# Two transformer blocks on one core: prologue by quarters, late modulation loads in pairs, norm weights in ScalarE's copies, first 1/sum behind v

## The chip, the cores and the metric

One core of a Trainium2 chip runs the whole program. It has five engines with a queue each: TensorE (matmuls; PE in the profile, PEld its weight loads), VectorE (DVE), ScalarE (ACT), GpSimd (POOL) and SyncE (SP), which here only starts transfers. The metric is the device time of one execution in microseconds (us); lower is better.

## The reference, cut to what matters

Two blocks on x of 256 tokens by 2048, all in fp32. The first begins with a modulation: a vector c times a matrix w_ada of 2048 by 12288 (100 MB) gives shift, scale and gate of two norms.

```
c_act = silu(c);  sh1, sc1, gt1, sh2, sc2, gt2 = split(c_act @ w_ada + b_ada, 6)
h = rms_norm(x, g_norm1) * (1 + sc1) + sh1
q_d, k_d, v_d, cq, ckv, k_pe = split(h @ w_in)
q_d = rms_norm(q_d, g_q_diff);  k_d = rms_norm(k_d, g_k_diff)          # heads of 64
p1, p2 = softmax(q1 k1 / 8 + bias), softmax(q2 k2 / 8 + bias)          # 8 heads
a_out = rms_norm((p1 - lam * p2) @ v_d, g_subln) * (1 - lambda_init)
q_m = rope_tail(rms_norm(rms_norm(cq, g_q_a) @ w_q_b, g_q_mla))        # 8 heads of 128 + 64
k_m, v_m = ... @ w_kv_b (the same, with g_k_mla and the shared k_pe)
x = x + gt1 * (concat(a_out, softmax(q_m k_m) v_m) @ w_out)
h2 = rms_norm(x, g_norm2) * (1 + sc2) + sh2
x = x + gt2 * ((silu(h2 @ w_gate) * (h2 @ w_up)) @ w_down)
```

The second block (convolution branch, attention with forget gates, feed-forward, final norm) follows.

## The kernel before, in words

**Units.** Every weight matrix is streamed in loads of 1 MB into a ring of four buffers (raw). Each load is two units. For a unit ScalarE rounds 128x1024 numbers to w_hi (split, L1120 and L1133), VectorE forms the rest w_lo (L1645), and TensorE does twelve matmuls of 512 columns: hi by hi, lo by hi, hi by lo (unit, L615, L628). Units go through four slots and are split up to three units ahead. The results stand in three accumulators (acc).

**Modulation.** w_ada is read in 96 loads of 1 MB. For the first 80, TensorE multiplies a load with the columns of c (a "part", L658: four matmuls on 32 partitions each). Parts belong to groups; a finished group is copied to SBUF by VectorE (L1691, L1695) and turned into columns by TensorE (L673, L676), and VectorE adds the bias (L1717 to L1724). SEGMENTS says by which pieces of the 2048 rows of h the first 32 parts (NPRO) are grouped: each piece needs a group of sh1 and one of sc1. LEAD parts stand ahead of the first unit. These 32 loads have a ring of their own with four buffers (early_ada, L468); the later 48 go through raw between the weights, where GAPS says how many follow each load of weights. Each of the later 48 takes a PSUM bank alone and is added by VectorE (L1699, L1701). There are two such banks, used in turn by all transposes, parts, columns and attention products: their order is fixed, and a bank is used again only when its last reader is done.

**Order.** Each engine's program is written out by hand, and all follow the same tables: `prologue()` (L107) for what stands ahead of the first unit, `modulation(u)` (L124) for parts and columns behind unit u, `window(v)` (L378) for attention steps behind a unit, `heads_at` for the second attention. Segment 0 is units 0 to 11 (rows 0 to 1023 of h), segments 1 and 2 are units 12 to 17 and 18 to 23. The last part of the prologue's groups releases GpSimd's load of the bias table (L1603), which the mirror matmuls (L777) behind unit 17 and later read.

**Attention.** `qkN` (L1932) scales queries and keys by 1/rms and then by the weight g; `qbN` and `kvbN` (L1971, L1997) do the same for the second attention, with the rotation. TensorE transposes the result into a bank and ScalarE copies it out (bank_to, L1169). For a head of the first attention ScalarE does the exponentials (daE), `daW` (L2031) forms 1/sum for both softmaxes, scales the second, and subtracts; `dc` (L2044) copies the product with v out of its bank, ScalarE squares it, and `dcN` (L2051) does the norm.

## Time and profile before

| | |
|---|---|
| median of 3 runs | 2698.8 us (2695.52 to 2700.94) |
| the profiled execution | 2699.22 us, its span 2697.4 us |
| mean granted TensorE clock | 0.990 |
| TensorE busy | 2615.0 us (97%), 12162 matmuls |
| VectorE, ScalarE, GpSimd busy | 1583.7 (59%), 1163.8 (43%), 52.8 (2%) us |
| moved by DMA | 561.74 MB, mean 208 GB/s |
| matmuls of L628 in the chain that ended last | 83% of the span |

The page of the profile has the busy time of each engine, the chain of work that ended last, and the costliest groups of instructions. A span of matmul records is pipelined: a busy TensorE is one with no pause, not one at its peak. The trace behind it gives single instructions with the time that an engine stood idle before them and who released it.

### The profile page before, as it was taken

How to read it: one execution, taken by the hardware profiler on the slowest of the kernel's cores; microseconds unless marked ns; L12 is line 12 of the kernel's file. 1: busy time of each engine (PE TensorE's matmuls, PEld its weight loads, DVE VectorE, ACT ScalarE, POOL GpSimd, SP SyncE). 2: the span in 40 equal slices, each digit the busy share in tenths (PEclk: the TensorE clock that was granted, in tenths of full speed). 3: DMA queues.
4: the chain of work that ended last, by engine and by line, in shares of the span. 5: the costliest groups of instructions: out<-in, count | busy, mean ns of one | idle time of the engine just before them, and what ended most of it. 6: DMA issues, size and time to landing. Idle time of an engine off the chain costs nothing.

```text
span 2697.4 us, 32987 instructions
## 1 busy us (share of the span) xinstructions
PE 2615.0 (97%) x12162; PEld 2083.3 (77%) x12162; DVE 1583.7 (59%) x1755; ACT 1163.8 (43%) x1514; POOL 52.8 (2%) x84
## 2 busy tenths in 40 slices
PE   6999879989999999999999999999999999999997
PEld 2667656778888888887888877888888888888886
DVE  1467665657777555557755454556556565656565
ACT  2344444444333444443544455444444444444443
POOL 1010010000000000000000000000000000000000
PEclk9999989989999999999999999999999999999999
DMA  9967766647777655555655544665655555555552
GB/s 390 378 229 261 271 233 231 217 137 250 248 245 245 195 187 187 188 190 188 214 188 184 175 141 145 200 209 203 208 191 187 191 191 192 187 187 187 190 190 103
DMA packets 262819, 561.74 MB, mean 208 GB/s; under 512 B 9186, under 2 KB 13492, under 8 KB 261836
## 3 DMA queue, kind: packets, MB, share of 16 engines
q1 hardware_dynamic: 260688, 549.25, 60.4%
q0 software_dynamic: 1664, 9.19, 1.0%
q10 hardware_dynamic: 380, 2.13, 0.2%
q8 instruction: 57, 0.93, 0.1%
q14 instruction: 30, 0.25, 0.0%
HBM read 556.31 MB, written 4.21 MB: 208 GB/s over the span
## 4 chain that ended last, share of the span: by engine, by line
PE 91%; DVE 4%; DMA 2%; ACT 1%; issue 1%; POOL 0%; DVEq 0%; SPq 0%; POOLq 0%; ACTq 0%
PE acc L628 83%; PE bank L712 2%; PE bank L658 2%; DMA early_mix<-in_w_ada 2%; DVE w_lo L1645 1%; PE bank L862 1%; ACT w_hi L1133 0%; PE acc L853 0%; PE acc L1062 0%; PE acc L852 0%; PE acc L1061 0%; PE bank L724 0%; PE bank L686 0%; ACT probs L1340 0%; PE bank L676 0%
## 5 line engine op out<-in xcount | busy, mean ns | idle before, releaser
L1645 DVE TENSOR_TENSOR w_lo<-raw,w_hi 128x1024 fp32r<-128x1024 f32 x852 | 1037.9, 1225 | 816.3 <-ACT w_hi L1133 784.5
L1133 ACT ACTIVATE w_hi<-raw 128x1024 fp32r<-128x1024 f32 x852 | 901.3, 1060 | 1061.3 <-PE acc L628 960.7
L628 PE MATMUL acc<-w_hi,actT_hi 128*128 128x512 f32 (+1 forms) x2112 | 834.7, 395 | 1.2 <-DVE actT_lo L1783 0.8
L628 PE MATMUL acc<-w_hi,actT_lo 128*128 128x512 f32 (+1 forms) x2112 | 821.7, 389 | 0.0
L628 PE MATMUL acc<-w_lo,actT_hi 128*128 128x512 f32 (+1 forms) x2112 | 821.5, 389 | 0.0
L628 PE MATMUL acc<-w_hi,mixT_hi 128*128 128x512 f32 (+1 forms) x1280 | 503.5, 393 | 8.5 <-DVE mixT_lo L1773 5.4
L628 PE MATMUL acc<-w_hi,mixT_lo 128*128 128x512 f32 (+1 forms) x1280 | 498.0, 389 | 0.0
L628 PE MATMUL acc<-w_lo,mixT_hi 128*128 128x512 f32 (+1 forms) x1280 | 497.2, 388 | 0.0
L628 PEld LDWEIGHTS acc<-w_hi,actT_hi 128*128 128x128 f32 x2112 | 397.9, 188 | 115.0 <-issue 25.8
L628 PEld LDWEIGHTS acc<-w_hi,actT_lo 128*128 128x128 f32 x2112 | 397.8, 188 | 83.0
L628 PEld LDWEIGHTS acc<-w_lo,actT_hi 128*128 128x128 f32 x2112 | 398.3, 189 | 79.0 <-issue 1.0
L628 PEld LDWEIGHTS acc<-w_hi,mixT_hi 128*128 128x128 f32 x1280 | 241.0, 188 | 72.1 <-issue 13.5
L628 PEld LDWEIGHTS acc<-w_hi,mixT_lo 128*128 128x128 f32 x1280 | 240.7, 188 | 49.6
L628 PEld LDWEIGHTS acc<-w_lo,mixT_hi 128*128 128x128 f32 x1280 | 241.0, 188 | 47.5
L2142 DVE TENSOR_TENSOR x_res<-x_res,acc 128x1024 f32<-128x1024 f32 x68 | 83.1, 1221 | 30.5 <-PE acc L628 30.5
L658 PE MATMUL bank<-raw,ccol 128*32 128x512 f32 x384 | 54.0, 641 | 11.7 <-DVEq L1722 5.6
L712 PE MATMUL bank<-cst,work 128*128 128x128 f32 x356 | 47.7, 273 | 11.0 <-DVEq L1705 3.9
L712 PEld LDWEIGHTS bank<-cst,work 128*128 128x128 f32 x356 | 41.5, 140 | 19.5 <-issue 6.3
L1180 ACT ACTIVATE mixT_hi<-bank 128x512 fp32r<-128x512 f32 (+1 forms) x54 | 25.6, 504 | 64.7 <-PE bank L712 40.6
L2142 DVE TENSOR_TENSOR wide<-wide,acc 128x1024 f32<-128x1024 f32 x36 | 44.0, 1221 | 14.5 <-PE acc L628 14.5
L1434 ACT ACTIVATE work<-acc,kpe 128x512 f32<-128x512 f32 x48 | 30.4, 686 | 39.3 <-PE acc L628 39.3
L1576 POOL TENSOR_SCALAR rstd<-ss 128x2 f32<-128x2 f32 (+2 forms) x27 | 7.6, 283 | 1965.6 <-DVE ss L1803 1713.7
(270 smaller groups left out, 1128.6 us busy)
## 6 DMA issues: line engine op xcount, KB each, us to landing
raw<-in_w_ff SPq DMA_DIRECT2D x128, 1024.0 KB, 5.1
raw<-in_w_in SPq DMA_DIRECT2D x108, 1024.0 KB, 5.1
raw<-in_w_ada SPq DMA_DIRECT2D x64, 1024.0 KB, 5.0
raw<-in_w_gate SPq DMA_DIRECT2D x44, 1024.0 KB, 5.1
raw<-in_w_up SPq DMA_DIRECT2D x44, 1024.0 KB, 5.1
raw<-in_w_down SPq DMA_DIRECT2D x44, 1024.0 KB, 5.0
early_mix<-in_w_ada SPq DMA_DIRECT2D x16, 1024.0 KB, 9.5
wide<-in_w_ada SPq DMA_DIRECT2D x16, 1024.0 KB, 8.8
```

The source lines that it names most:

```text
L628: last_mm = pe.matmul(acc[p][:, t, 0:width], act[x][:, k0 + c, t * P:(t + 1) * P], w[:, u % SPL, c * NW:c * NW + width], start=first and c ...
L658: ins = pe.matmul(dst[32 * j:32 * j + 32, :], ccol[:, 2 * r + j // 2 if n_ == 8 else 4 * r + j, :], src[:, j * NW:(j + 1) * NW], start=alo ...
L712: ins = pe.transpose(bank[b][:, j * P:(j + 1) * P], src_of(j), ident)
L862: ins = pe.matmul(bank[b][:, 0:S], v[:, k, h * P:(h + 1) * P], attT[:, k, :], start=(k == 0), stop=(k == 1))
L1133: act.activation(w_hi[:, u % SPL, :], raw[:, ld % RAW, (u % DU) * 1024:(u % DU + 1) * 1024], ACT.Copy) \
L1180: act.activation(dst, bank[b][:, 0:n], ACT.Copy).then_inc(bank_hi, 1)
L1434: ins = act.activation(stg[:, t * NW:(t + 1) * NW], acc[p][:, t, :], ff, scale=scale[:, t:t + 1])
L1576: link(pool.tensor_scalar(slot, ss[:, 0:n], 1.0 / width, EPS, ALU.mult, ALU.add))
L1645: dve.tensor_tensor(w_lo[:, u % SPL, :], raw[:, ld % RAW, (u % DU) * 1024:(u % DU + 1) * 1024], w_hi[:, u % SPL, :].bitcast(F32), ALU.subt ...
L2142: link(dve.tensor_tensor(dst[:, :, g * NW:(g + 1) * NW], dst[:, :, g * NW:(g + 1) * NW], acc[g % 2][:, :, :], ALU.add))
```

## The change

Six edits. (1) The first segment is halved, so that four segments of 512 rows each are left: LEAD falls from 16 to 8, a segment is six units, and behind its units 0 to 3 stand 1, 2, 2 and 3 parts of the next one; SyncE asks for 3, 3 and 2 of these behind each load of weights. The copies of gains, the transposes of x, the first splits and the modulation of the first columns are mixed in one list. (2) The later 48 parts come as 24 pairs, spread over loads 12 to 50; a pair adds up in one bank and VectorE takes it once. (3) The weights of the norms of queries and keys are no longer multiplied in by VectorE: ScalarE's copy out of the bank takes them as its scale, and the rotated part has them in its tables (turns_q). (4) The first softmax is left unscaled: the weights become p1 + p2 * (-lam * sum1 / sum2), and 1/sum1 comes with the norm behind v. (5) The product with v is copied by ScalarE, after its squares, and no longer by VectorE. (6) b_f_2 is loaded apart, later, by GpSimd.

```diff
-SEGMENTS = ((0, 8), (8, 4), (12, 4))
+SEGMENTS = ((0, 4), (4, 4), (8, 4), (12, 4))
-GAPS = [0] * 12 + [1] * 16 + [2] * 9 + [1] * 14 + [0] * 3
+EARLY_GAPS = (3, 3, 2)
+EARLY_AT = (1, 2, 2, 3, 0, 0)
+GAPS = [0] * 12 + [2 * ((i + 1) * 24 // 39 - i * 24 // 39) for i in range(39)] + [0] * 3
@@ prologue()
-        if 5 <= a < 13:
-            steps.append(("x", 2 * (a - 5)))
-        if a == 13:
-            steps.append(("gains",))
-        if a == 14:
-            steps.append(("rows",))
-    steps += [("columns", n) for n in completed(LEAD - 1)]
-    return steps + [("part", LEAD), ("part", LEAD + 1)]
+        if a == 3:
+            steps += [("gains",), ("rows",)]
+        if a >= 4:
+            steps.append(("x", 2 * (a - 4)))
+    steps += [("x", 8), ("columns", 1), ("modulated", 0), ("split",), ("split",), ("x", 10), ("modulated", 1)]
+    return steps + [("x", 12), ("x", 14), ("split",)]
@@ modulation(u)
-        return [LEAD + 1 + v] if 0 < v < NPRO - LEAD - 1 else []
+        if not 0 <= v < 18:
+            return []
+        first = LEAD + v // 6 * 8 + sum(EARLY_AT[:v % 6])
+        return list(range(first, first + EARLY_AT[v % 6]))
@@ TensorE, part_sums
+                begins, ends = (r == 0, r == n_ - 1) if a < NPRO else (a % 2 == 0, a % 2 == 1)
...
-                                    src[:, j * NW:(j + 1) * NW], start=alone or r == 0,
-                                    stop=alone or r == n_ - 1)
+                                    src[:, j * NW:(j + 1) * NW], start=begins, stop=ends)
@@ ScalarE
-            def bank_to(dst, n=NW, shape=None):
+            def bank_to(dst, n=NW, shape=None, weight=None):
...
-                act.activation(dst, src, ACT.Copy).then_inc(bank_free[b], 1)
+                scale = 1.0 if weight is None else cols2[:, ROWS2[weight][0]:ROWS2[weight][0] + 1]
+                act.activation(dst, src, ACT.Copy, scale=scale).then_inc(bank_free[b], 1)
@@ ScalarE, dc
-                skip_banks(1)
-                act.wait_ge(oc_ready, h + 1)
+                b = next_bank()
                 before_sums()
                 for t in range(TT):
-                    ins = act.activation(sq[:, t * P:(t + 1) * P], ostg[:, t, :], ACT.Square, accum_out=ss[:, t:t + 1])
+                    ins = act.activation(sq[:, t * P:(t + 1) * P], bank[b][:, t * P:(t + 1) * P], ACT.Square,
+                                         scale=rr[:, t:t + 1], accum_out=ss[:, t:t + 1])
                 ins.then_inc(ss_ready, 1)
+                act.activation(ostg.rearrange("p t d -> p (t d)"), bank[b][:, 0:TT * P], ACT.Copy) \
+                    .then_inc(bank_free[b], 1)
@@ VectorE, part_sums
-                if a < NPRO and not last_of_group(a):
+                if (a < NPRO and not last_of_group(a)) or (a >= NPRO and a % 2 == 0):
                     return
@@ VectorE, qkN; qbN; kvbN
-                g_ = (gq, gk)[g // 2][:, :].unsqueeze(1).broadcast_to([P, 16, 64])
-                dve.tensor_tensor(stg.rearrange("p (a d) -> p a d", d=64), stg.rearrange("p (a d) -> p a d", d=64), g_,
-                                  ALU.mult).then_inc(stg_ready, 1)
...
-                link(dve.tensor_tensor(s4, s4, gqm[:, :].unsqueeze(1).broadcast_to([P, 4, QKH]), ALU.mult))
...
-                free(p)
-                dve.tensor_tensor(s4, s4, gkm[:, 0:P].unsqueeze(1).broadcast_to([P, 4, P]), ALU.mult)
...
                 dve.wait_ge(stg_ready, L.next("stg"))
+                free(p)
                 inv_rms_used()
@@ VectorE, daW
-                link(dve.tensor_scalar(rr[:, 2:4], rr[:, 2:4], lam[:, 0:1], None, ALU.mult))
-                for t in range(TT):
-                    ins = dve.tensor_scalar(probs[:, 2 + t, :], probs[:, 2 + t, :], rr[:, 2 + t:3 + t], None, ALU.mult)
-                link(ins)
-                for t in range(TT):
-                    ins = dve.scalar_tensor_tensor(out=attw[:, t, :], in0=probs[:, t, :], scalar=rr[:, t:t + 1],
-                                                   in1=probs[:, 2 + t, :], op0=ALU.mult, op1=ALU.subtract)
+                link(dve.scalar_tensor_tensor(out=rr[:, 2:4], in0=rr[:, 2:4], scalar=lam[:, 0:1], in1=rs[:, 0:2],
+                                              op0=ALU.mult, op1=ALU.mult))
+                for t in range(TT):
+                    ins = dve.scalar_tensor_tensor(out=attw[:, t, :], in0=probs[:, 2 + t, :], scalar=rr[:, 2 + t:3 + t],
+                                                   in1=probs[:, t, :], op0=ALU.mult, op1=ALU.add)
@@ VectorE, the first 24 units
-                for q in modulated_at(u - 1):
+                for q in modulated_at(u):
```

How TensorE's queue changes ahead of the first unit. L658 (now L665) is a part, L724 (L730) a transposed pair of x, L673 and L676 (L682) the columns of a group, L770 (L775) the gains, L628 (L635) a matmul of a unit. Before, from product 12 on (L757 is the turning of the second set of rows):

```order
L658 MATMUL acc<-early_mix,ccol 32x512 x4
L724 MATMUL bank<-rt,x_res 128x128 x4
L658 MATMUL acc<-early_mix,ccol 32x512 x4
L770 MATMUL bank<-probs,ones 128x512
L770 MATMUL bank<-probs,ones 128x392
L658 MATMUL acc<-wide,ccol 32x512 x4
L757 MATMUL bank<-cst,tmp 128x104
L658 MATMUL acc<-wide,ccol 32x512 x4
L673 MATMUL bank<-sel,part 128x2 x4
L658 MATMUL bank<-early_mix,ccol 32x512 x8
L628 MATMUL acc<-w_hi,actT_hi 128x512
```

and now, from product 5 on:

```order
L665 MATMUL acc<-early_mix,ccol 32x512 x4
L730 MATMUL bank<-rt,x_res 128x128 x4
L665 MATMUL acc<-wide,ccol 32x512 x4
L730 MATMUL bank<-rt,x_res 128x128 x4
L665 MATMUL acc<-wide,ccol 32x512 x4
L730 MATMUL bank<-rt,x_res 128x128 x8
L682 MATMUL bank<-ones,part 128x1 x4
L730 MATMUL bank<-rt,x_res 128x128 x12
L635 MATMUL acc<-w_hi,actT_hi 128x512
```

Sixteen products and the first two of the next group (L658 into bank, x8) stood ahead of the first unit; now eight do, and three of the eight transposed pairs stand behind the columns.

SyncE's queue, where the late loads of w_ada go through the ring raw. Before, where w_in ends:

```order
L451 DMA raw<-in_w_in 128x4x512
L451 DMA raw<-in_w_ada 128x2x1024
L451 DMA raw<-in_w_in 128x4x512
L451 DMA raw<-in_w_ada 128x2x1024
L451 DMA raw<-in_w_in 128x4x320
L451 DMA raw<-in_w_ada 128x2x1024 x2
L451 DMA raw<-in_w_in 128x4x320
```

and now:

```order
L458 DMA raw<-in_w_in 128x4x512 x2
L458 DMA raw<-in_w_ada 128x2x1024 x2
L458 DMA raw<-in_w_in 128x4x512
L458 DMA raw<-in_w_in 128x4x320
L458 DMA raw<-in_w_ada 128x2x1024 x2
L458 DMA raw<-in_w_in 128x4x320
L458 DMA raw<-in_w_ada 128x2x1024 x2
```

Before, one load of w_ada followed each load of weights, and two followed each of nine; now it is two or none all through, with one or two loads of weights between (here one load of 512 columns and one of 320 stand together).

VectorE's queue at a head of the first attention with the norm of keys: L2034 to L2040 are daW (now L2030 to L2034), L1936 and L1942 are qkN (now L1937 alone), L1701 (L1706) the sum of a part, L1645 (L1653) a w_lo. Before:

```order
L1701 TENSOR_TENSOR part<-part,bank 128x512
L1645 TENSOR_TENSOR w_lo<-raw,w_hi 128x1024
L1936 TENSOR_TENSOR work<-acc,rstd 128x1024
L1942 TENSOR_TENSOR work<-work,gains 128x1024
L2034 RECIPROCAL rr<-rs 128x4
L2035 TENSOR_SCALAR rr<-rr,lam 128x2
L2037 TENSOR_SCALAR probs<-probs,rr 128x256 x2
L2040 SCALAR_TENSOR_TENSOR att<-probs,rr 128x256 x2
L1645 TENSOR_TENSOR w_lo<-raw,w_hi 128x1024
L1773 TENSOR_TENSOR mixT_lo<-bank,mixT_hi 128x256
L1701 TENSOR_TENSOR part<-part,bank 128x512
```

and now:

```order
L1653 TENSOR_TENSOR w_lo<-raw,w_hi 128x1024 x2
L1937 TENSOR_TENSOR work<-acc,rstd 128x1024
L2030 RECIPROCAL rr<-rs 128x4
L2031 SCALAR_TENSOR_TENSOR rr<-rr,lam,rs 128x2
L2034 SCALAR_TENSOR_TENSOR att<-probs,rr 128x256 x2
L1653 TENSOR_TENSOR w_lo<-raw,w_hi 128x1024
L1778 TENSOR_TENSOR mixT_lo<-bank,mixT_hi 128x256
L1706 TENSOR_TENSOR part<-part,bank 128x512
```

The product with the weights, the two scalings of the second softmax and the sum of a part ahead are gone from here; the sum behind is left (L1773, now L1778, is the low half of a finished head).

## Rows read from the trace of the kernel before

**Rows 1.** Windows by stretch: us, busy (x instructions) of each engine, PEclk, DMA share, GB/s.

```profile
60.00:133.00 73.00, 72.96 (x369) 46.88 (x370) 31.20 (x42) 27.95 (x35) 1.01 (x1) 0.97 1.01 386
...
280.00:345.00 65.00, 54.94 (x360) 38.81 (x359) 44.88 (x79) 27.83 (x76) 5.77 (x11) 0.95 0.79 279
345.00:410.00 65.00, 49.17 (x248) 32.42 (x247) 44.22 (x86) 30.20 (x102) 10.69 (x17) 0.89 0.66 229
410.00:500.00 90.00, 88.94 (x428) 60.96 (x427) 46.03 (x79) 36.70 (x69) 0.00 (x0) 1.00 0.67 230
```

**Rows 2.** The chain of waits: start, us, engine, tile and line.

```profile
61.98 7.02 PE acc L628 x24
...
70.00 2.95 PE acc L628 x12
...
122.67 1.00 PE bank L658 x8
...
126.62 0.79 PE bank L676 x8
...
154.31 5.67 PE acc L628 x24
```

**Rows 3.** Timeline ahead of the first unit: start, us, instruction, idle before it.

```profile
31.98 1.07 PE L658 MATMUL acc<-wide,ccol 128*32 128x512 f32 x8
...
32.97 1.16 PE L724 MATMUL bank<-rt,x_res 128*128 128x128 f32 x8
...
39.89 1.06 PE L658 MATMUL acc<-wide,ccol 128*32 128x512 f32 x8 [0.30 <-DMA wide<-in_w_ada]
...
42.33 1.06 PE L658 MATMUL acc<-wide,ccol 128*32 128x512 f32 x8 [0.29 <-DMA wide<-in_w_ada]
...
44.52 0.60 ACT L1174 ACTIVATE xT<-bank 128x512 f32<-128x512 f32 x1 [1.85 <-PE bank L724]
...
54.78 2.00 ACT L1133 ACTIVATE w_hi<-raw 128x1024 fp32r<-128x1024 f32 x2 [7.22 <-DMA raw<-in_w_in]
...
56.69 1.08 ACT L1251 ACTIVATE xT<-xT,mcol 128x256 f32<-128x256 f32 x2
```

**Rows 4.** The page's DMA issues: size of each, median us to landing.

```profile
raw<-in_w_ada SPq DMA_DIRECT2D x64, 1024.0 KB, 5.0
```

**Rows 5.** Timeline: the issue of the bias table, and the first mirror matmul.

```profile
124.72 1.01 POOL L1603 DMA_DIRECT2D wide<-bias_by_distance  x1 [103.46 <-DVE part L1695]
...
132.84 1.02 PE L777 MATMUL bank<-wide,att 128*128 128x512 f32 x2
```

**Rows 6.** The tile of the bias table, 110 to 140 us: from issue to landing.

```profile
DMA to landing us min/median/max: 7.2/7.2/7.2
```

**Rows 7.** VectorE's groups by shape, 165 to 410 us: busy us, mean ns; idle before.

```profile
L1701 DVE TENSOR_TENSOR part<-part,bank 128x512 f32<-128x512 f32 x31 | 21.2, 685 | 7.2 <-PE bank L658 5.7
...
L2037 DVE TENSOR_SCALAR probs<-probs,rr 128x256 f32<-128x256 f32 x16 | 4.9, 351 | 0.3
```

**Rows 8.** Timeline near 200 us: the weights of the keys, and TensorE behind them.

```profile
199.28 1.23 DVE L1942 TENSOR_TENSOR work<-work,gains 128x1024 f32<-128x1024 f32 x1 [0.24 <-DVE work L1936]
...
204.04 1.22 PE L712 MATMUL bank<-cst,work 128*128 128x128 f32 x8 [1.23 <-DVE mixT_lo L1773]
```

**Rows 9.** The chain of waits near 364 us.

```profile
364.52 0.97 DVE work L1983
```

**Rows 10.** Windows of 2 us, columns as in rows 1.

```profile
320.00:322.00 2.00, 0.00 (x0) 0.00 (x0) 1.76 (x6) 0.00 (x0) 0.00 (x0) 0.54 1.02 383
322.00:324.00 2.00, 1.96 (x9) 0.33 (x9) 0.69 (x1) 0.97 (x1) 0.00 (x0) 0.50 1.05 416
```

**Rows 11.** Timeline: two parts that came together, and their sums.

```profile
310.64 1.92 PE L658 MATMUL bank<-raw,ccol 128*32 128x512 f32 x16
...
315.44 1.51 DVE L1701 TENSOR_TENSOR part<-part,bank 128x512 f32<-128x512 f32 x2
```

**Rows 12.** Waits from 340 to 400 us: us in total, times, longest.

```profile
PEld bank L658 <- DMA raw<-in_w_ada: 2.8, 2, 1.8
```

More of the change, by code:

```diff
@@ L453, in load @@
                 if kind == "w":
-                    for _ in range(2):
+                    for _ in range(EARLY_GAPS[(ORDER[:n[0]].count("w") - 1) % 3]):
                         if asked[0] < NPRO:
@@ L765, in gain_columns @@
             def gain_columns():
[L767 to L771 removed]
+                pe.wait_ge(gain_in, 16 * 4)
+                b, _ = wait_bank()
+                pe.matmul(bank[b][:, 0:NW], ones[0:1, :], gains_row[:, 0:NW], start=True, stop=True) \
+                    .then_inc(bank_full[b], 1)
             def mirror_chunk(n_):
```

143 lines of the change are left out of this document (68 added, 75 removed).

## Prediction

> **What bounds the kernel now.** The page first: TensorE is busy for 97% of the span, as the table of the profile shows, so only three things can save time: work taken from TensorE, a start that comes sooner, and pauses that close. The windows by stretch say where pauses are [rows 1]. From 410 to 500 us, and from 500 on as well, TensorE hardly stops. From 280 to 410 it is busy 54.94 of 65 and 49.17 of 65 us, so 25.9 us of pause lie there, while VectorE has 44.88 and 44.22 us of work in the same stretches; the granted clock falls to 0.95 and 0.89 too. The chain of waits says how the run starts: loads of the modulation matrix until 61.98 us, when the first two units run (a unit is 12 matmuls of 128x512), then a steady pattern: product of a part 1.00, unit 2.95, and 0.79 for turning a finished group into columns [rows 2]. In that stretch the DMA engines are full (share 1.01, 386 GB/s) and TensorE is too (72.96 of 73 us) [rows 1].
>
> **Prologue by quarters.** Eight products instead of sixteen now stand ahead of the first unit, and the two of the next group that stood there are gone as well. Before, product 7 ran at 31.98 and took 1.07 [rows 3], so it ends at 33.0; now it is the last one needed. Behind it stand two transposed pairs at 1.05 (1.16 with the overlap) and the columns, 1.0: 36.2. VectorE turns these into the scale, 0.7; ScalarE then does two of its 128x256 products (1.08), two w_hi copies (2.00) and one bank copy (0.60), which frees the bank that the last transposed pair waits for: 40.6, and 1.2 for the pair. First unit at 41.9, 20 us sooner [rows 2, 3]. Most of this is work that only changes places: from there a segment of six units carries eight products and two columns. Six units are four at 2.95 and two at 2.72 (a unit behind a unit is cheaper: two behind a product take 5.67 [rows 2]), products 8 x 1.0, columns 2 x 0.79: 26.8 us. Product 31 ends after two segments, four units, eight products and one group of columns: 41.9 + 53.6 + 20.6 = 116.1.
>
> The loads need about the same: a load of 1 MB comes each 2.45 us (the products at 39.89 and 42.33, each waiting for its load) [rows 3], eleven per segment are 27.0. And the four early buffers are used harder: load 15 may be asked for only when product 11 is done (three units and four products, 54.8), takes 5.0 alone [rows 4] and more behind another, so it lands at 60 to 62, while TensorE comes to it at 61.5. I take 1.1 us of wait in each of three segments: product 31 ends at 119.5. Now a new wait shows. GpSimd asks for the bias table when the last part is summed; before, its issue stood at 124.72, 1.05 behind product 31 (ended 123.67), and it landed 7.2 later [rows 2, 5, 6], 8.3 us after the product. The mirror matmul at 132.84 found it there, having three units and columns between (9.2 us) [rows 5]. Now two units and columns stand between: 6.7 us, so TensorE waits 1.6 and the mirror runs at 127.8, 5.0 sooner than before. Half a us I take back for the clock of the first units and for the shorter path from a segment's last columns to its next unit, two units less than before. Term: -4.5. Ends: -8 (no wait on loads, table landed), +1 (load waits of 3 us in each segment).
>
> **ScalarE takes the norm weights.** The copy out of the bank (0.60 for 512 columns [rows 3]) gets a scale, which I price at nothing: it replaces a constant in the same instruction (ends 0 and 0.1 us each). VectorE loses one 128x1024 product of 1.23 for each of four groups [rows 8], one 128x768 of 0.97 for each of four query pairs [rows 9], and one 128x512 of 0.69, the size of a sum [rows 7], for each of four key pairs. The first kind decides once: at 199.28 it runs, and at 204.04 TensorE has stood 1.23 us waiting for that row of VectorE's work [rows 8]. Term: -1.2 (ends 0, -1.3). Elsewhere before 280 TensorE has cover enough.
>
> **1/sum behind v.** Each of eight heads loses two scalings of 351 ns [rows 7] with their wait; the bank copy moves to ScalarE, +0.4 for each head ahead of its next w_hi (256 columns; bounds 0.3, half of the 0.60, and 0.6), and is no longer waited for before the squares.
>
> **The stretch 280 to 410.** The chain there runs through VectorE, row by row; the 0.97 us of the query weights at 364.52 is one such row [rows 9]. On the chain stand four of these (-3.9), three heads' scalings (3 x 0.7 = -2.1), and two second sums of a part (2 x 0.8 = -1.6). The pairs also take products away: of 48 parts 18 stood at units 54 to 70, now 12. Six products less of 1.0 on a path that they share half of the time: -3.0. Against it ScalarE's longer step twice (+0.8) and the later release of the key sums (+0.6, since now the bank is given back behind three VectorE operations). -9.2 in all; other paths come forward where a chain is cut, and I take two thirds: -6.0. Ends: 0 and -14.
>
> **Late loads in pairs.** The six products go where TensorE is the bound. There a lone product costs 1.0 and makes the next unit dearer by 0.23, a pair costs 2.15. Units 22 to 52: 16 x 1.2 = 19.2 before, 9 x 2.15 + 0 = 19.4 now; units 72 to 98: 14 x 1.2 = 16.8, now 19.4. Term: +2.7 (ends +1, +5). VectorE does 24 sums instead of 48 of 0.69 [rows 7], hidden here behind 88.94 of 90 us of matmuls [rows 1].
>
> **Sum.** -4.5 -1.2 -6.0 +2.7 = -9.0. The profiled execution took 2699.2 us (the span of 2697.4 and 1.8 around it), 0.4 above the median of the runs. 2690.
>
> **Rivals.**
> The stretch opens (B). VectorE has 12 sums less (8.3), four query weights (3.9), four key weights (2.8), five heads' scalings (3.5) and bank copies (1.6), 20 of its 89 us there; the pauses may go below the point where the clock falls. The clock means 0.95 and 0.89 over 65 us each are 10.4 us of full-speed cycles [rows 1]; a window at 0.50 stands there [rows 10]. If two thirds of this come back and the cut chain counts in full, it is -9.2 and -7 in place of -6: 2680. For it: VectorE is the bound there for many rows of the chain. Against: ScalarE and GpSimd steps stand on the same chain and stay.
> The Trainium skill (TensorE: Matmul & The Clock Gate, "Part 1: The HAM clock gate") says that an idle TensorE is throttled to half rate and that activity releases it. By that rule, shorter pauses pay twice; the trace agrees, the 0.50 follows a window without any matmul [rows 10].
>
> Little is left (C). The loads set the pace: at the mean 386 GB/s of 60 to 133 us instead of 430, a load of 1.05 MB takes 2.72, the 33 loads behind product 7's end at 122 at the earliest, 2.5 later, and the stretch gives only half: -2, -1.2, -3, +2.7: 2696. For it: DMA share 1.01. Against: the same engines brought a load each 2.45 us at 40 us [rows 3].
> The Trainium skill (DMA: Bandwidth & Descriptors, "Bandwidth") puts HBM to SBUF at about 358 GB/s for a core. An estimate by that page of the Trainium skill is 2.93 us for a load, 33 of them 97 us, and the mirror at 138, 5 us later than before. The measured 386 to 430 contradict it, so it gets no chance of its own.
>
> Slower (D): the pairs starve. Where two pairs follow each other (nine places: units 28/30, 38/40, 44/46, 54/56, 64/66, 70/72, 80/82, 90/92, 96/98) the second part of the second pair can be asked for only when the first pair is summed, and part and sum are now released together. It lands 5.0 + 0.5 behind the sum [rows 4]; TensorE has two units (5.7), one product (1.0) and at least 1 us of head work until it needs it, 7.7. It decides when the sum comes more than 2.2 us behind the pair. Where VectorE is free the sum ends 0.7 behind its product, but the two sums at 315.44 end at 316.95, 4.4 behind their products (312.56) [rows 11]; the longest wait of the weights of a product for its load is 1.8 there [rows 12]. Nine times 1.8 are 16: 2706. For it: VectorE's order. Against: only two or three of the nine lie where VectorE is late, and there it is relieved.
>
> **Chances.** Forecast 0.50, B 0.25, C 0.16, D 0.07, others 0.02. What the measurement tells from no change is 0.2%, 5.4 us. Faster than 2693.4: most of the forecast (0.46), B and a little of C: 0.74. The same: 0.18. Slower: 0.08. The range for 8 in 10 holds forecast, C and nearly all of B: 2676 to 2699.
>
> **What would show it.** First unit at 41 to 43 us (wrong above 46). TensorE waits for an early load once in each segment, near 1 us; over 3 means C. The first mirror matmul waits for the bias table, 1 to 3 us, and runs at 126 to 130. No wait of TensorE for w_lo near 200. From 280 to 410: pauses of 15 to 20 instead of 25.9 us; below 12 with the clock at 0.97 or more means B. Waits of TensorE for raw loads from w_ada of more than 5 us in all mean D. Behind 550 us nothing should differ by more than 1 us; if it does, the forecast has left something out.

## The result, and the profile after

| | before | after |
|---|---|---|
| median | 2698.34 us (2695.52 to 2700.94) | 2709.78 us (2706.27 to 2712.43) |
| ratio, 95% interval | | 1.0042 [1.0029, 1.0055] |
| the profiled execution, its span | 2699.22, 2697.4 | 2706.27, 2704.2 |
| first matmul of the first unit | 61.91 | 42.19 |
| first product of group 2 (behind unit 0) | | 45.12 |
| first mirror matmul | 132.84 | 155.3 |
| first matmul of w_kv_b (L905 before, L910 after) | 371.3 | 374.3 |
| first transpose of the second norm | 546.5 | 553.7 |

The change made the kernel 0.42% slower, 11.4 us by the medians and 7.0 by the two profiled executions. The table of times shows three parts: 22.5 us are lost up to the mirror matmul, 19.5 won from there to w_kv_b (238.5 us before, 219.0 after), 4.2 lost again up to the second norm. Behind that the two differ by 0.4 us in all: the span ends 6.8 us later. The kernel before was run again beside every set of experiments; its median was 2698.34 us here, and 2699.91 (e1 to e4), 2700.47 (e5 to e8), 2699.22 (e9 to e12) and 2699.32 (e13 to e15) later, so a difference between two sets can be off by 2 us.

The first table is the windows of the kernel after, with the stretches of [rows 1] (us, busy and instructions of PE, PEld, DVE, ACT, POOL, then granted clock, DMA share and GB/s).

```profile
60.00:133.00 73.00, 60.65 (x304) 35.83 (x304) 23.65 (x32) 18.67 (x24) 0.00 (x0) 0.91 0.86 317
280.00:345.00 65.00, 62.60 (x393) 48.09 (x392) 44.98 (x74) 35.39 (x82) 5.75 (x10) 1.00 0.76 266
345.00:410.00 65.00, 52.00 (x284) 38.49 (x283) 37.87 (x81) 35.38 (x122) 12.83 (x22) 0.92 0.68 231
410.00:500.00 90.00, 90.00 (x447) 62.91 (x444) 43.16 (x74) 37.49 (x71) 0.00 (x0) 1.00 0.70 252
```

From 60 to 133 us TensorE was busy for 72.96 of 73 us before [rows 1] and is for 60.65 now, and the DMA engines, full before (1.01), are at 0.86. Neither TensorE nor the loads bound this stretch any more: something makes both wait. From 280 to 410 the pauses are 15.4 us instead of 25.9. These windows are fixed in time while the work in them has moved by some us, so a part of the difference may be the shift.

Next, the timeline of TensorE ahead of the first unit, the counterpart of [rows 3]. The last transposed pair ends at 42.4, and the first unit begins at 42.19: forecast 41.9.

```profile
36.05 1.02 PE L682 MATMUL bank<-ones,part 128*128 128x1 f32 x8
36.93 2.03 PE L730 MATMUL bank<-rt,x_res 128*128 128x128 f32 x16
41.27 1.16 PE L730 MATMUL bank<-rt,x_res 128*128 128x128 f32 x8 [2.31 <-ACT xT L1180]
45.12 1.07 PE L665 MATMUL bank<-early_mix,ccol 128*32 128x512 f32 x8
```

Then the timeline of SyncE (SPq: its queue; start, time until all of the row are issued, waits within the row included, line), and of the other engines in the same place. L488 are early loads of w_ada, L458 loads of weights, L1704 is VectorE's copy of a finished group, L682 TensorE's columns of it.

```profile
50.60 0.51 SPq L458 DMA_DIRECT2D raw<-in_w_in  x1
51.15 12.27 SPq L488 DMA_DIRECT2D wide<-in_w_ada  x2
63.47 0.51 SPq L458 DMA_DIRECT2D raw<-in_w_in  x1
```
```profile
58.98 2.00 ACT L1138 ACTIVATE w_hi<-raw 128x1024 fp32r<-128x1024 f32 x2 [11.79 <-DMA raw<-in_w_in]
60.07 2.36 DVE L1653 TENSOR_TENSOR w_lo<-raw,w_hi 128x1024 fp32r<-128x1024 f32 x2 [11.44 <-ACT w_hi L1138]
62.35 0.68 DVE L1704 COPY part<-bank 128x512 f32<-128x512 f32 x1
63.23 1.35 PE L682 MATMUL bank<-ones,part 128*128 128x1 f32 x8 [4.42 <-DVEq L1710]
70.69 2.01 ACT L1138 ACTIVATE w_hi<-raw 128x1024 fp32r<-128x1024 f32 x2 [9.71 <-DMA raw<-in_w_in]
```

This is the loss. Read it from the bottom up: ScalarE waits 9.71 us for weights that SyncE asked for only at 63.47. In front of them in SyncE's queue stood early load 15 (the second of the two that begin at 51.15), whose buffer product 11 had used. Product 11 is the last of its group, so SyncE waits for VectorE's copy of the sum, not for the product. That copy (62.35) stands on VectorE behind w_lo of units 4 and 5 (60.07), and w_lo waits for weights that landed late (58.98), since SyncE asked for them only at 50.60, behind early load 13, which waits for product 9 in unit 1. So a late load of weights delays the copy, the copy delays the next load, and that one comes late again. From 60 to 63 us no matmul runs and almost nothing is transferred (10 GB/s), as the window shows:

```profile
60.00:63.00 3.00, 0.00 (x0) 0.00 (x0) 2.93 (x3) 0.98 (x2) 0.00 (x0) 1.00 0.02 10
```

The waits of SyncE from 40 to 155 us (us in total, times, longest), and the two sides that pay for them:

```profile
SPq L488 <- PE bank L665: 44.1, 10, 9.4
SPq L488 <- DVE part L1704: 39.7, 5, 11.4
```
```profile
ACT w_hi L1138 <- DMA raw<-in_w_in: 70.3, 9, 11.8
PE bank L682 <- DVEq L1710: 16.1, 6, 4.4
```
```profile
SPq L481 <- PE bank L658: 24.5, 8, 4.8
SPq L481 <- DVE part L1695: 12.9, 3, 4.3
```

The last two lines are the kernel before: the same wait for the copy is there, three times, never over 4.3 us. After, the wait comes at each group's end. The first products of the segments stand at 45.12, 81.58 and 117.46, 36 us apart. GpSimd asks for the bias table at 145.6 (124.72 in [rows 5]), it takes 9.6 us to land (7.2 in [rows 6]), and the mirror matmul waits for it, 2.8 us, until 155.3.

### The profile page after: what moved, and what is told of

Same layout as the page of the kernel before. It is cut to its first block, busy times and chain, and to the rows that moved or that the text cites. A ratio compares the mean times of both kernels' runs of the same rounds, so it can differ in the third digit from the quotient of the medians.

```text
span 2704.2 us, 33011 instructions
## 1 busy us (share of the span) xinstructions
PE 2616.4 (97%) x12176; PEld 2091.4 (77%) x12176; DVE 1550.7 (57%) x1711; ACT 1167.0 (43%) x1522; POOL 53.8 (2%) x86
## 4 chain that ended last, share of the span: by engine, by line
PE 83%; DVE 2%; ACT 1%; issue 1%; DMA 0%; POOL 0%; DVEq 0%; POOLq 0%; ACTq 0%
PE acc L635 77%; PE bank L718 2%; PE bank L665 1%; PE bank L867 1%; DVE w_lo L1653 0%; PE acc L858 0%; PE acc L1067 0%; PE acc L857 0%; PE acc L1066 0%; PE acc L910 0%; PE bank L730 0%; DMA raw<-in_w_ada 0%; PE bank L692 0%; DVE wide L2162 0%; DVE x_res L2166 0%
## 5 line engine op out<-in xcount | busy, mean ns | idle before, releaser
L1653 DVE TENSOR_TENSOR w_lo<-raw,w_hi 128x1024 fp32r<-128x1024 f32 x852 | 1037.6, 1225 | 874.0 <-ACT w_hi L1138 843.5
L635 PE MATMUL acc<-w_hi,actT_hi 128*128 128x512 f32 (+1 forms) x2112 | 835.6, 396 | 1.7 <-DVE actT_lo L1788 0.8
L635 PE MATMUL acc<-w_hi,actT_lo 128*128 128x512 f32 (+1 forms) x2112 | 822.9, 390 | 0.0
L635 PE MATMUL acc<-w_lo,actT_hi 128*128 128x512 f32 (+1 forms) x2112 | 822.6, 389 | 0.0
L635 PE MATMUL acc<-w_hi,mixT_hi 128*128 128x512 f32 (+1 forms) x1280 | 503.9, 394 | 9.6 <-DVE mixT_lo L1778 4.3
L635 PE MATMUL acc<-w_hi,mixT_lo 128*128 128x512 f32 (+1 forms) x1280 | 498.3, 389 | 0.0
L635 PE MATMUL acc<-w_lo,mixT_hi 128*128 128x512 f32 (+1 forms) x1280 | 497.8, 389 | 0.0
L635 PEld LDWEIGHTS acc<-w_hi,actT_hi 128*128 128x128 f32 x2112 | 398.3, 189 | 104.7 <-issue 19.8
L635 PEld LDWEIGHTS acc<-w_hi,actT_lo 128*128 128x128 f32 x2112 | 398.1, 188 | 83.1
L635 PEld LDWEIGHTS acc<-w_lo,actT_hi 128*128 128x128 f32 x2112 | 398.6, 189 | 80.1 <-issue 1.5
L635 PEld LDWEIGHTS acc<-w_hi,mixT_hi 128*128 128x128 f32 x1280 | 241.1, 188 | 70.1 <-issue 13.1
L635 PEld LDWEIGHTS acc<-w_hi,mixT_lo 128*128 128x128 f32 x1280 | 241.1, 188 | 49.5
L635 PEld LDWEIGHTS acc<-w_lo,mixT_hi 128*128 128x128 f32 x1280 | 241.4, 189 | 47.5
L665 PE MATMUL bank<-raw,ccol 128*32 128x512 f32 x384 | 47.4, 600 | 8.2 <-DMA raw<-in_w_ada 5.8
L1682 DVE SCALAR_TENSOR_TENSOR part<-raw,ccol,part 128x512 f32<-128x512 f32 x60 | 45.1, 751 | 1.7
```

Source lines behind the costliest of these rows:

```text
L635: last_mm = pe.matmul(acc[p][:, t, 0:width], act[x][:, k0 + c, t * P:(t + 1) * P], w[:, u % SPL, c * NW:c * NW + width], start=first and c ...
L665: ins = pe.matmul(dst[32 * j:32 * j + 32, :], ccol[:, 2 * r + j // 2 if n_ == 8 else 4 * r + j, :], src[:, j * NW:(j + 1) * NW], start=beg ...
L1653: dve.tensor_tensor(w_lo[:, u % SPL, :], raw[:, ld % RAW, (u % DU) * 1024:(u % DU + 1) * 1024], w_hi[:, u % SPL, :].bitcast(F32), ALU.subt ...
L1682: ins = dve.scalar_tensor_tensor(out=part[:, :], in0=src, scalar=ccol[:, k, 0:1], in1=part[:, :], op0=ALU.mult, op1=ALU.add)
```

## Experiments

**The two halves of the change.** The first run puts the prologue of before into the changed kernel, the second the new prologue alone into the kernel before:

```diff
-SEGMENTS = ((0, 4), (4, 4), (8, 4), (12, 4))      # e1; e2 is the reverse
+SEGMENTS = ((0, 8), (8, 4), (12, 4))
-EARLY_GAPS, EARLY_AT = (3, 3, 2), (1, 2, 2, 3, 0, 0)
+EARLY_GAPS = (2, 2, 2);  early(v) = [LEAD + 1 + v] if 0 < v < NPRO - LEAD - 1 else []
```

> The changed kernel with the prologue of before put back (one group pair of 8 chunks, then two of 4; 16 early products ahead of the first unit; two early loads behind each weights load); norm weights, softmax change and pairs of late loads stay. Theory T (the new prologue holds itself up: SyncE's early load waits for VectorE's copy of a finished group, the copy stands behind w_lo, w_lo waits for a weights load that SyncE only asks for behind that early load): the mirror row is back near 132.8 us from 155.3, and all behind it keeps its gain over before, so about 2687 us (2683 to 2690). Rival T2 (the stretch from the mirror to 371 us gained 19.5 us only because it had fallen behind and caught up with loads that had run ahead): the mirror is back too, but behind it only some 7 us are gained and 4 lost, about 2695 us (2692 to 2698). Rival R (the prologue was not the loss): 2705 us or more.

Measured 2684.87 us, ratio to before 0.9945 [0.9932, 0.9959]. The mirror is back at 132.9, and the stretch to w_kv_b takes 218.4 us, as in the changed kernel (219.0). T holds; T2 falls, the gain behind the mirror is no catching up. The changed kernel is 24.9 us above this one by the medians, 26.5 if each is held against the kernel before of its own set.

> The kernel before with the new prologue alone (quarters, weights mixed in, three, three and two early loads behind each weights load); late loads single, norm weights on VectorE, softmax as before. Theory T, the parts simply add: mirror row near 155, 2698 + 22 = 2720 us (2716 to 2723). Rival T2 (a late prologue is partly caught up between the mirror and 371 us whatever the rest is): mirror near 155, but 2708 us (2705 to 2712). Rival R (the prologue was not the loss): 2690 to 2699.

Measured 2730.44, ratio 1.0119 [1.0103, 1.0134]: 30.5 us over before, mirror at 161.0, 5.7 later still than in the changed kernel. T's sign and place hold, its range (2716 to 2723) does not: "simply add" was too low by 10 us. The rest of the change takes 4 to 6 us off what this prologue costs. Which part does was not tried.

**The links of the circle, one at a time.** Order on VectorE's queue (e3), release of the early buffer (e4), order on SyncE's queue (e5):

```diff
@@ e3: VectorE, unit(), for the first 17 units
-                split();  run(todo);  modulation events
+                run(todo);  modulation events;  split()
@@ e4: SyncE, early_ada(), where product `used` is the last of its group
-                        sp.wait_ge(part_ready, sums_by(used))
+                        sp.wait_ge(bank_full[b], m)        # the product itself
@@ e5
-EARLY_GAPS = (3, 3, 2)
+EARLY_GAPS = (3, 1, 4)
```

> The changed kernel, but in the first 17 units VectorE takes a unit's modulation work (the copy of a finished group, the columns) ahead of the split of the unit three further on, instead of behind it. Theory T: the copy no longer waits for a weights load that SyncE asks for behind the early load that waits for the copy; SyncE's waits for that copy fall from 39.7 us to under 10, a segment takes some 28 us instead of 36, mirror row near 130, 2684 to 2692 us. Rival L (the loads themselves set the pace of the prologue, 28 MB asked in another order): segments stay near 36 us, mirror over 150, 2706 us or more.

Measured 2703.36, 1.0010 [0.9999, 1.0020]: 6.4 us better than the changed kernel, mirror 147.7. Outside T's range, and not L's either. By the order of the code it removes one step only: in unit 1 the split of unit 4 already stands ahead of unit 2's copy, and both halves of a load wait for the same landing. No run tried that alone. SyncE's waits for the copy fell to 30.9 us, where T had said under 10:

```profile
SPq L488 <- DVE part L1708: 30.9, 5, 10.4
```

> The changed kernel, but an early load whose buffer was last read by the last product of a group waits for that product (its bank being full) instead of for VectorE's copy of the sum; the copy itself stays behind w_lo. Theory T: this cuts the circle at its other link, so the weights loads come on time and w_lo with them; the copy is then late only by the units that VectorE splits ahead; SyncE waits for products only, mirror row 130 to 140, 2685 to 2697 us. Rival Q (the order on VectorE's queue is the whole cost, SyncE's wait only follows it): mirror over 148, 2703 us or more. Rival L (the loads' own pace): 2706 or more.

Measured 2701.83, 1.0010 [1.0000, 1.0019], mirror 147.5: 8.0 us better, at the poor end between T and Q. The wait for the copy is gone from SyncE, but the waits for products grew from 44.1 to 70.0 us:

```profile
SPq L489 <- PE bank L666: 70.0, 14, 10.3
```

TensorE's columns still wait for the copy behind w_lo (11.0 us in all, 16.1 in the changed kernel), and the third weights load of a segment stands behind load 13, which waits for product 9.

> The changed kernel with one table altered: behind the weights loads of a segment 3, 1 and 4 early loads are asked instead of 3, 3 and 2, so the third weights load no longer stands behind early load 13, which waits for product 9 in the second unit. Theory T, widened by what the two runs before showed (each of the two cuts alone gave 7 us): SyncE asks the third weights load of each segment only at 50.6 us and it lands near 60, when unit 4 wants it; asked 12 us earlier, that stall of 4 to 6 us in each of three segments goes, the circle by the copy may still hold the next load: mirror 134 to 146 instead of 155, 2687 to 2699 us. Rival L (DMA bytes set the pace): 2705 or more.

Measured 2693.11, 0.9972 [0.9962, 0.9982], 16.7 us better and in T's range: two early loads moved from ahead of the third load of weights to behind it are worth more than either cut. Mirror 144.9, in a profiled execution that was the slowest of nine (2701.02). The wait for the copy is still there, five times, but no longer than 4.3 us:

```profile
SPq L488 <- DVE part L1704: 21.0, 5, 4.3
```

**All three, and whether quarters gain at all.**

> The changed kernel with all three repairs: early loads asked 3, 1 and 4 behind the weights loads, VectorE's modulation work ahead of its split in the first 17 units, and the early load released by the product rather than by VectorE's copy. Theory T: with no wait left that goes through a load asked later, the prologue by quarters gives what the prediction gave it: mirror 126 to 131, 2679 to 2685 us, some 5 us below the run with the old prologue. Rival L (in the kernel before the DMA share is 1.01 from the start to 123 us, so the loads bound the prologue in either order): mirror 131 to 135 and 2684 to 2689, no better than the old prologue. Rival S (a fourth wait is behind these): over 2692.

Measured 2686.67, 0.9944 [0.9931, 0.9956]; the mirror stands at 138.4 in the profiled execution, which took 2694.4 and was the slowest of the five. By its time that is L, not T; the mirror is later than either said. To settle it, three kernels ran on one chip, this one again, one with 3, 2, 3 in the table, and the old prologue again:

> The kernel with all three repairs, but early loads asked 3, 2 and 3 behind the weights loads of a segment instead of 3, 1 and 4. In the trace of the 3, 1, 4 run the DMA queue runs dry once, share 0.26 and 0.32 in the two stretches 48 to 51 and 51 to 54 us, because every load that needed no product had been asked by then; 3, 2, 3 leaves one more early load ahead of the third weights load. Theory D (the prologue by quarters is bound by its bytes: 28.4 us a segment for 11 loads of 1 MB, so only dry stretches can be won): mirror within 3 us of the 3, 1, 4 run and 2683 to 2688 us. Theory C (the circle returns through early load 12, which waits for product 8 ahead of the third weights load): 2690 or more.

> The kernel with all three repairs once more, beside the one with the old prologue on the same chip. Theory Q (quarters, once repaired, gain what the prediction gave them, 4.5 us): 4 us or more below the old prologue. Theory D (bytes bind both): within 3 us of it, and the mirror row no more than 2 us earlier than 132.9 us.

> The changed kernel with the prologue of before, once more, beside the one with all three repairs on the same chip: 2683 to 2687 us by every theory, mirror at 132.9; it is the base that the other two are held against.

Measured 2688.33 (0.9964 [0.9950, 0.9978], mirror 134.4), 2684.94 (0.9949 [0.9935, 0.9962], mirror 130.8) and 2682.16 (0.9942 [0.9929, 0.9956], mirror 132.7). Q falls: the repaired quarters reach the mirror 1.9 us sooner than e15 and gain nothing in the end, 2.8 us above the old prologue with intervals that overlap. D's time is met and its mirror limit, 2 us before 132.9, missed by 0.1. Its reason, the bytes, is only a part of it, as the rows of e14 below show. The 3, 2, 3 run lies just between D and C by its time and its mirror. The dry stretch it was to close is in it as well (share 0.47 from 45 to 48 us) and is missing in e14, so it belonged to one execution and not to the order.

The profiled executions differ in when their first unit starts, for a reason of its own (see "What the runs showed of the hardware"). From there to the mirror (us):

| | first unit | mirror | between |
|---|---|---|---|
| forecast | 41.9 | 127.8 | 85.9 |
| the changed kernel | 42.2 | 155.3 | 113.1 |
| e2, new prologue alone | 45.0 | 161.0 | 116.0 |
| e3, copy first | 42.2 | 147.7 | 105.5 |
| e4, early released | 41.2 | 147.5 | 106.3 |
| e5, weights earlier | 47.2 | 144.9 | 97.7 |
| e6, all three | 46.8 | 138.4 | 91.6 |
| e13, all three, 3, 2, 3 | 43.2 | 134.4 | 91.2 |
| e14, all three again | 40.7 | 130.8 | 90.1 |

So e6, e13 and e14 are alike within 1.5 us, and the place of one early load (3, 2, 3 or 3, 1, 4) makes no difference that shows. The timeline and a window of e14:

```profile
43.67 1.07 PE L666 MATMUL bank<-early_mix,ccol 128*32 128x512 f32 x8
...
72.05 1.06 PE L666 MATMUL bank<-early_mix,ccol 128*32 128x512 f32 x8
...
100.15 1.07 PE L666 MATMUL bank<-early_mix,ccol 128*32 128x512 f32 x8
```
```profile
60.00:133.00 73.00, 64.02 (x351) 39.76 (x348) 29.25 (x42) 22.83 (x30) 1.00 (x1) 0.97 1.04 405
```

The first product of each segment comes 28.4 and 28.1 us behind the last, with eleven loads of 1.05 MB in between: 409 GB/s, and the window shows a share of 1.04 at 405 GB/s. TensorE is nearly full too: from 43.67 to 100.15 it is busy for 54.0 of 56.5 us. It waits for an early load once in each segment, 1.0 us each time, 3.0 in all, which is what the forecast gave a segment (26.8 us of work and 1.1 of wait). Of the 9 us of pause in the window most is one wait for the bias table:

```profile
119.73 1.00 POOL L1611 DMA_DIRECT2D wide<-bias_by_distance  x1 [99.77 <-DVE part L1709]
130.79 2.07 PE L783 MATMUL bank<-wide,att 128*128 128x512 f32 x2 [5.46 <-DMA wide<-bias_by_distance]
```

GpSimd asks for the table at 119.73, 4.8 us sooner than in e15 (124.57) and 0.8 sooner than forecast. But the table takes 11.0 us to land (11.3 in e6, 11.0 in e13), against 7.2 in e15. So 3.8 of the 4.8 us are lost in its landing. The DMA engines are fuller while it is under way, a share of 1.04 from 119.7 to 130.8 us against 0.85 in e15 from 119.0 to 132.7; that this makes the landing longer fits, but no run changed it alone. The last 1.9 us are gone at the second norm: from w_kv_b to there e14 takes 183.0 us, e15 179.4. In e6 and e13 it is 179.6 and 179.3, so this belongs to the one execution. The Trainium skill (DMA: Bandwidth & Descriptors, "Bandwidth") puts HBM to SBUF at about 358 GB/s for a core while both cores of a pair stream, and at 425 for one core alone with 16 MB; an estimate from the first is 32.2 us for a segment's eleven loads. The run, a program on one core, has 28.2, which is nearer to the second.

**Where the gain behind the mirror is from.** The pairs taken out of e1, and put alone into the kernel before:

```diff
-GAPS = [0] * 12 + [1] * 16 + [2] * 9 + [1] * 14 + [0] * 3          # before; e7
+GAPS = [0] * 12 + [2 * ((i + 1) * 24 // 39 - i * 24 // 39) for i in range(39)] + [0] * 3
-    start, stop = True, True; one bank and one addition for each late part
+    start, stop = a % 2 == 0, a % 2 == 1; one bank and one addition for two      # e8
```

> The first of these runs (changed kernel, prologue of before) with the late modulation loads single again, in the places of before, each product with its own bank and its own addition. Theory P+ (pairs cost, the prediction's +2.7: their first loads wait for the pair's sum): 2682 us (2680 to 2684). Theory P- (pairs gain: one pass of VectorE fewer per two loads, 24 of 685 ns, and banks open for less): 2690 us or more. 2684 to 2687 means that they do nothing.

> The kernel before with the late loads in pairs alone (places and sums), prologue, norm weights and softmax as before. Theory P+: 2702 us (2700 to 2704). Theory P-: 2695 or less. If P- holds on one base and P+ on the other, the pairs are worth something only where VectorE is the late party, which the norm weights and the softmax change relieve as well.

Measured 2699.56 (0.9995 [0.9986, 1.0004]) and 2690.23 (0.9963 [0.9950, 0.9976]). P- holds on both bases: the pairs are worth 10.2 us alone (medians 2690.23 and 2700.47) and 14.7 with the rest (e1 against e7, of two sets; 14.1 against the kernel before of each), while norm weights and softmax without them are worth nothing that can be measured. Three runs take the pairs apart, the first two with one bank and one addition per part:

```diff
@@ e9: pair places, single sums
+GAPS as in e8;  everything else as before
@@ e10: single sums, spread evenly
+GAPS = [0] * 12 + [(i + 1) * 48 // 39 - i * 48 // 39 for i in range(39)] + [0] * 3
@@ e11: the pairs of e8, VectorE
+                    ins = dve.tensor_tensor(part[:, :], part[:, :], part[:, :], ALU.max)
```

> The kernel before, with only the places of the late modulation loads changed to those of the pairs (two behind one weights load, 24 times, spread over 39 weights loads); every product keeps its own bank and its own addition on VectorE. The pairs as a whole, alone on this base, gave 2690.2 against 2700.5. Theory Pl (the gain is the spreading: before, nine loads in a row carry two, in the stretch that ends near 330 us): 2690 to 2694 us. Theory Su (the gain is the shared bank and the pass of VectorE that is saved): 2698 us or more.

> The kernel before, with its 48 late loads spread evenly over 39 weights loads, one or two behind each, and single sums. Theory Pl: 2690 to 2694 us, like the pair places. Theory Su: 2697 to 2702. Rival E (two loads behind one weights load are what hurts, wherever): evenly spread singles below the pair places by 2 us or more.

> The pairs alone on the kernel before, and VectorE makes one more pass of 128x512 per pair (the maximum of the sum with itself, in place), so it makes as many passes as with single sums, while the bank is still filled once per pair. Theory V (the pass saved is the gain, since VectorE is late for TensorE between 280 and 410 us): 2697 us or more. Theory Bk (the bank taken once instead of twice, or the places): 2690 to 2693 us.

Measured 2698.70 (0.9999 [0.9990, 1.0008]), 2694.94 (0.9981 [0.9972, 0.9989]) and 2688.10 (0.9959 [0.9948, 0.9971]). V falls, Su holds for e9, and E for e10; e11 is 2 us below the range of Bk. VectorE's saved passes are worth nothing that shows: e11 makes as many as before and is as fast as e8. The places alone are worth nothing either, two single sums behind one load undo what the spreading gives (E: evenly spread singles are 3.8 better). What is left between e9 and e11, which have the same places and the same number of passes, is 10.6 us for what the shared bank brings: it is taken once instead of twice, and VectorE stops once, behind the second product. These two were not taken apart. The busy time and idle time of TensorE's products from the mirror to w_kv_b, before, e9 and e11:

```profile
L658 PE MATMUL bank<-raw,ccol 128*32 128x512 f32 x272 | 38.2, 643 | 10.5 <-DVEq L1722 5.6 <-DVE mixT_lo L1773 2.3 <-ACT q_nope L1174 1.7
```
```profile
L658 PE MATMUL bank<-raw,ccol 128*32 128x512 f32 x240 | 30.8, 615 | 8.9 <-DVE mixT_lo L1773 7.4 <-DMA raw<-in_w_ada 0.9 <-ACT x_res L1174 0.3
```
```profile
L660 PE MATMUL bank<-raw,ccol 128*32 128x512 f32 x240 | 29.4, 599 | 2.8 <-DMA raw<-in_w_ada 2.3 <-ACT x_res L1175 0.3
```

With a bank for each part, a product waits until VectorE has emptied the bank it takes next (5.6 and 2.3 us before, 7.4 in e9). With one bank for two, that wait is gone in e11 and 1.1 us in e8; what remains is the load. The transposes, which take banks from the same two, do not gain but wait a little longer. TensorE's waits in this stretch for a bank that VectorE had to empty, in us:

| | before | e9 | e8 | e11 |
|---|---|---|---|---|
| products of parts | 7.9 | 7.4 | 1.1 | 0 |
| transposes | 7.4 | 7.8 | 8.9 | 9.1 |

The whole stretch from mirror to w_kv_b, in one window each, of before, e9, e8 and e11:

```profile
132.80:371.30 238.50, 217.71 (x1194) 153.18 (x1194) 165.86 (x254) 106.70 (x232) 27.39 (x32) 0.97 0.73 255
```
```profile
132.60:364.10 231.50, 211.97 (x1155) 155.34 (x1154) 161.40 (x248) 107.11 (x236) 27.10 (x32) 0.96 0.68 243
```
```profile
132.50:356.70 224.20, 208.48 (x1155) 151.56 (x1154) 152.16 (x233) 106.64 (x232) 26.27 (x32) 0.98 0.71 252
```
```profile
133.50:356.20 222.70, 208.79 (x1156) 154.21 (x1154) 160.89 (x247) 106.58 (x232) 27.43 (x32) 0.98 0.72 253
```

Of the 14.3 us between before and e8, 9.2 are busy time of TensorE (30 products instead of 34 stand there, 30.8 us instead of 38.2) and 5.1 are pause, as much as the table gives. The four products are not saved: they come behind w_kv_b, where e8 takes 3.4 us more up to the second norm, so 10.9 are left, near the 10.2 of the medians.

The two traces of e9 and e11 need care. The one of e9 is of its fastest execution of eleven (2695.06), the one of e11 of the second slowest of six (2694.76, where four took 2685.6 to 2689.8), and their spans are equal, 2693.3 and 2693.0 us. What e11 gains up to w_kv_b, 8.8 us, it loses from there to the second norm: 185.5 us at a granted clock of 0.94, against 178.7 at 0.98 in e9 and 178.6 at 0.97 in e8. The 10.6 us stand on the medians. Whether the added pass causes the slow executions of e11 stays open.

**Softmax or norm weights.** Edits (4) and (5) of the change on top of e8:

```diff
-attw = p1 * rr1 - (p2 * rr2);  dc copied by VectorE, then squared
+attw = p1 + p2 * rr2';  dc squared by ScalarE from the bank with scale rr1, then copied by it
```

> The pairs alone plus the change to the first softmax (1/sum behind v, ScalarE squares and copies dc's bank); norm weights stay on VectorE. With norm weights as well the run gave 2684.9, with the pairs alone 2690.2. Theory X (the softmax change carries these 5 us, it shortens the heads' chain): 2684 to 2687 us. Theory N (the norm weights carry them): 2689 to 2691 us.

Measured 2686.14, 0.9955 [0.9942, 0.9967]: inside X's range, 4.1 us below e8 and 1.3 above e1, but the three intervals overlap. In the traces the stretch from mirror to w_kv_b is 224.2, 221.4 and 218.4 us with the pairs alone, with softmax, and with both.

## Why the prediction was wrong

**Prologue by quarters: -4.5 forecast, +22.5 at the mirror.** This is the step that failed. The first unit came as worked out (42.2 for 41.9), with luck in it, since eight executions with this prologue have it between 40.7 and 47.2. The arithmetic of a segment, 26.8 us for TensorE and 27.0 for the loads, was near the 28.2 that the repaired kernel takes. What failed is "I take 1.1 us of wait in each of three segments": a segment took 36.5 and 35.9 us. The prediction saw that load 15 needs product 11, and put its issue at 54.8. It was issued behind 62.35, because SyncE waits for VectorE's copy. Neither that copy's place behind w_lo nor what stands behind load 15 in SyncE's queue (the next weights) was followed: the wait for the copy, 39.7 us of SyncE's time in all, was put at nothing without a reason. The loss is three waits linked through two queues written in order: cutting one gave 6 to 17 us, all three 23 and 25.

Repaired, the term is nought: 2684.94 against 2682.16. There the waits for loads are as forecast (1.0 us a segment) and product 31 ends at 118.7, forecast 119.5. The step that failed is the landing of the bias table, taken as 7.2 us from the kernel before: it took 11.0, TensorE waited 5.5 us for it instead of 1.6, and the mirror stood at 130.8, not 127.8. The loads' rate, read at 40 us as one each 2.45, was 2.56 in the segments (28.2 by 11).

**Norm weights: -1.2.** Right at its place, not told from nothing in the time. The rows are the transposes of the same keys in e12 (weights still on VectorE), in e1 and in the changed kernel; [rows 8] has 1.23 us of wait before them.

```profile
203.86 1.22 PE L713 MATMUL bank<-cst,work 128*128 128x128 f32 x8 [1.20 <-DVE mixT_lo L1773]
202.97 1.22 PE L716 MATMUL bank<-cst,work 128*128 128x128 f32 x8
227.37 1.22 PE L718 MATMUL bank<-cst,work 128*128 128x128 f32 x8 [0.54 <-DVE mixT_lo L1778]
```

The wait is gone in e1; in the changed kernel, where all stands later, 0.54 us are left, so the sign "no wait near 204" was met only in part. By the medians e1 and e12 differ by 1.3 us, within the spread.

**The stretch 280 to 410: -6.0 forecast, with -1.2 that is 7.2; 19.5 measured from the mirror to w_kv_b.** The direction was right and the pause as forecast (15.4 us, "15 to 20 instead of 25.9"; e1 has 15.4 too, e8 18.2), but that the number came out was luck, since the reason was not right. Nearly all was put to VectorE's shorter work. By itself that is worth 0.9 us (e7). What counted, the product that waits for its bank (5.6 and 2.3 us in the row of before above), was in the trace and in no term; the prediction had only "two second sums" of it on its chain. With the pairs in place norm weights and softmax bring 5.4 us more (e8 to e1, of two sets).

**Late loads in pairs: +2.7 forecast, -10.2 measured.** The term counted what the pairs cost where TensorE is the bound, and there its size was right: from w_kv_b to the second norm before took 175.2 us and e8 178.6, +3.4 (the term had +2.6 for units 72 to 98). It took nothing for the stretch ahead of it, except six products at half price. The missing part is the 14.3 us there.

**Rivals.** B's clock came back in part (1.00 and 0.92), but pauses below 12 us did not. C's sign, load waits of over 3 us in a segment, did not come: 1.0 each in e14, and product 31 ended at 118.7, where C had 122 at the earliest. Its mechanism, full DMA engines, is there (share 1.05), but the rate was 407 GB/s and not the 386 it took. D, the pairs starve, did not happen to a degree that counts: TensorE waits 5.8 us in all for raw loads of w_ada between 133 and 550 us, five times, at most 1.8 (0.4 before). That is over the 5 us that were to mean D, but far from its 16, and the pairs gain with it. D had named a wait of the loads for VectorE's sum, which is what made the kernel slower, but sought it in the pairs, the part that gained most. No rival had it in the prologue. Behind 550 us nothing differs, as said.

**Put together**: prologue +24.9 (after against e1), pairs -14.7 (e1 against e7), the rest -0.9 (e7 against before): +9.3, against 11.4 measured. The sum is no test: each step starts where the last ended, and the 2.1 us between are what the median of the kernel before differs by in the two sets. The version that beats both is e1, the change without its first edit: 2684.87 and 2682.16 us in two sessions, 0.9945 and 0.9942 of before.

## What to carry to other kernels

When a change makes a queue of loads wait for a buffer's last user, name who signals that use, what stands ahead of the signaller in its own queue, and what stands behind the waiting load in the queue of loads. If that path comes back to the same load, it is a circle that turns every late landing into the next one, and cheap only as long as loads are asked several units ahead.

Where two buffers are used in turn by all, count how often an operation takes one, not only how long its reader works: here one taking for two products gave 10 us, and giving the reader its saved work back cost nothing that shows.

Before pricing an earlier start, divide the bytes that must land up to the end of the stage by the rate with a full queue, and price the last transfer of the stage at the load it will then meet. Here a start 20 us sooner brought the last product 4.8 us sooner, and 3.8 of these went into the longer landing of the table behind it.

## What the runs showed of the hardware

The same kernel (e6 and e14, on two chips) began its first unit at 46.8 us in one profiled execution and at 40.7 in the other. The loads are not the reason: from 10 to 41 us TensorE waits 6.1 us for them in the one and 6.2 in the other, and from 24 to 30 us both move 408 to 410 GB/s. TensorE itself was slower. The rows are products 4, 5 and 7, first in e6, then in e14:

```profile
25.40 1.94 PE L666 MATMUL acc<-early_mix,ccol 128*32 128x512 f32 x8
30.98 1.94 PE L666 MATMUL acc<-early_mix,ccol 128*32 128x512 f32 x8
37.03 1.06 PE L666 MATMUL acc<-wide,ccol 128*32 128x512 f32 x8
```
```profile
24.15 1.07 PE L666 MATMUL acc<-early_mix,ccol 128*32 128x512 f32 x8
27.32 1.07 PE L666 MATMUL acc<-early_mix,ccol 128*32 128x512 f32 x8
31.66 1.07 PE L666 MATMUL acc<-wide,ccol 128*32 128x512 f32 x8
```

A product takes 1.94 us where the other execution takes 1.07. In e5, whose first unit begins at 47.2, products 4 and 5 take 1.94 us as well, and the window reads a granted clock of 0.56 there, which is mostly the lower of the two levels:

```profile
20.00:35.00 15.00, 13.53 (x55) 6.47 (x51) 3.51 (x13) 0.60 (x1) 0.00 (x0) 0.56 1.05 409
```

In e6 the clock column reads 1.00 at this place, against the length of the instructions, so durations must be read beside it. When TensorE rises to the upper level differs from one execution to the next, and the prologue by quarters pays for it: its first unit stands between 40.7 and 47.2 us in eight profiled executions. With the old prologue, whose later products wait for loads anyway [rows 3], it stands between 61.4 and 61.9 in nine. The profiled executions of e5 and e6, with the two latest first units, were also the slowest of nine and of five; the five of e6 took 2682.2 to 2694.4 us. In the executions without a profile the start was not seen, so how much of the spread is this stays open.
